# Sharing the exponents of the decays between GpSimd and VectorE, by block of columns

## What is computed

```python
# SSD, one direction:
acum = cumsum(dt * A)                            # per head
seg  = exp(where(mask, acum[l] - acum[s], NEG))  # decay from token s to token l
y    = einsum(C B^T, seg, x*dt)
# mLSTM, one direction:
dmat = where(mask, b[t] - b[s] + i[s], NEG)
m_t  = maximum(b[t] + m, max_s dmat)
sc   = (q k^T) * exp(dmat - m_t)
h    = (sc v) / maximum(|sum sc|, exp(-m_t))
```

## Time and profile before

| | |
|---|---|
| median of 3 runs | 2776.45 us (2774.89 to 2777.18) |
| profiled execution, its own time | 2774.36 us |
| its span | 2772.6 us |
| TensorE matmul / weight load busy | 91% / 83% |
| VectorE, ScalarE, GpSimd busy | 65%, 52%, 11% |
| mean granted TensorE clock | 0.959 of full speed |

### The profile page before, as it was taken

How to read it: one execution, slowest core, us unless ns; L and a number is a source line. 1 busy time by engine, 2 the same in 40 slices (tenths; PEclk the granted TensorE clock), 3 DMA queues, 4 the chain that set the end, 5 groups by cost and what they waited for, 6 DMA issues and landing times.

```text
span 2772.6 us, 42149 instructions
## 1 busy us (share of the span) xinstructions
PE 2532.0 (91%) x17296; PEld 2310.7 (83%) x17296; DVE 1790.0 (65%) x2816; ACT 1431.5 (52%) x2077; POOL 314.8 (11%) x299
## 2 busy tenths in 40 slices
PE   8998999999989997978998989998978998989997
PEld 7887989878789896977996888996978996888986
DVE  4556676565666655567666676874667666676864
ACT  4546545455564543555554535654555554535653
POOL 0000000000000000000229400000000229400000
PEclk9999999999999999989999989999989998999999
DMA  6543455555335565523566435664523465435663
GB/s 224 162 142 94 146 176 192 193 159 149 113 109 190 161 193 168 149 85 107 149 187 162 141 122 164 191 200 151 151 82 110 146 187 162 141 123 168 193 196 110
DMA packets 358670, 426.24 MB, mean 154 GB/s; under 512 B 21176, under 2 KB 286862, under 8 KB 358478
## 3 DMA queue, kind: packets, MB, share of 16 engines
q1 hardware_dynamic: 342602, 401.95, 47.0%
q10 hardware_dynamic: 14068, 15.91, 2.5%
q0 software_dynamic: 1808, 5.69, 0.6%
HBM read 422.35 MB, written 1.15 MB: 153 GB/s over the span
## 4 chain that ended last, share of the span: by engine, by line
PE 69%; DVE 14%; ACT 7%; issue 4%; POOL 4%; DMA 2%; ACTq 0%; DVEq 0%; POOLq 0%
PE ps L112 66%; POOL sE L124 3%; ACT whi L118 3%; DVE wlo L121 3%; PE ps L115 2%; ACT hgKm L118 1%; DVE sE L121 1%; DVE hgA L148 1%; ACT E L118 1%; DVE hgQB L121 1%; DVE hgQF L121 1%; DVE hgkf L121 1%; DVE hgkb L121 1%; DVE E L124 1%; ACT L118 0%
## 5 line engine op out<-in xcount | busy, mean ns | idle before, releaser
L121 DVE TENSOR_TENSOR wlo<-wring,whi 128x1024 fp32r<-128x1024 f32 x768 | 932.7, 1227 | 630.9 <-ACT whi L118 630.4
L118 ACT ACTIVATE whi<-wring 128x1024 fp32r<-128x1024 f32 x768 | 801.6, 1052 | 439.0 <-PE ps L112 428.7
L112 PE MATMUL ps<-uT,whi 128*128 128x256 f32 x4896 | 879.8, 284 | 23.2 <-DVE uT L121 23.2
L112 PEld LDWEIGHTS ps<-uT,whi 128*128 128x128 f32 x4896 | 761.1, 192 | 31.2 <-issue 24.0
L112 PE MATMUL ps<-uT,wlo 128*128 128x256 f32 (+1 forms) x2448 | 688.3, 281 | 0.0
L112 PEld LDWEIGHTS ps<-uT,wlo 128*128 128x128 f32 (+1 forms) x2448 | 469.3, 192 | 0.0
L112 PE MATMUL ps<-xT,whi 128*128 128x256 f32 x2112 | 382.0, 285 | 0.3 <-DVE wlo L121 0.3
L112 PEld LDWEIGHTS ps<-xT,whi 128*128 128x128 f32 x2112 | 327.1, 191 | 6.4 <-issue 3.7
L112 PE MATMUL ps<-xT,wlo 128*128 128x256 f32 x1056 | 296.7, 281 | 0.0
L112 PE MATMUL ps<-whi,hid 128*128 128x512 f32 x864 | 269.0, 391 | 0.0
L112 PEld LDWEIGHTS ps<-xT,wlo 128*128 128x128 f32 x1056 | 201.2, 190 | 0.1
(11 more groups left out here) (369 smaller groups left out, 3590.6 us busy)
## 6 DMA issues: line engine op xcount, KB each, us to landing
wring<-in_w_in SPq DMA_DIRECT2D x346, 512.0 KB, 3.7
wring<-in_mlp_w SPq DMA_DIRECT2D x128, 512.0 KB, 4.3
wring<-in_w_up SPq DMA_DIRECT2D x88, 512.0 KB, 4.4
wring<-in_w_down SPq DMA_DIRECT2D x44, 512.0 KB, 4.4
wring<-in_w_branch SPq DMA_DIRECT2D x32, 512.0 KB, 3.4
wring<-in_w_out SPq DMA_DIRECT2D x32, 512.0 KB, 3.8
wring<-in_mem_w_kv SPq DMA_DIRECT2D x16, 512.0 KB, 5.4
wring<-in_w_br_ssd SPq DMA_DIRECT2D x16, 512.0 KB, 3.8
```

The costliest lines, as they stand in the source:

```text
L112: return self.e.matmul(*p, **k) if self.e else Nothing()
L118: return self.e.activation(*p, **k) if self.e else Nothing()
L121: return self.e.tensor_tensor(*p, **k) if self.e else Nothing()
```

## The change

The four (with the mask's two: six) GpSimd instructions of a head become two (three): it does the two blocks of 256 columns. The two diagonal blocks of 128 are done by VectorE, in new functions `ssd_decay` and `ml_decay` of its program, which the list calls at the same steps. They record an event of their own, `arg2`, and ScalarE's exponential waits for both. The spread's DMA, too, waits for both before it writes over a piece. The mask of mLSTM is one constant of 256 columns, which GpSimd adds in one instruction, and VectorE takes in the same `scalar_tensor_tensor` as the column.

```diff
@@ schedule, decays of ssd_scan and ml_scan
-                c.spread[h].freed = ("arg", l, h)
+                c.spread[h].freed = [("arg", l, h), ("arg2", l, h)]
...
-                c.spread[16 + h].freed = ("arg", l, 16 + h)
+                c.spread[16 + h].freed = [("arg", l, 16 + h), ("arg2", l, 16 + h)]
@@ scalar_program
-        for ev in [s.before] if s.before else [("stored", c.l), ("storedmax", c.l), ("emraw", c.l)]:
+        for ev in s.before or [("stored", c.l), ("storedmax", c.l), ("emraw", c.l)]:
...
     def ssd_decay(c, h, s, r):
         e.wait_ge(*at(("arg", c.l, h)))
+        e.wait_ge(*at(("arg2", c.l, h)))
         e.activation(s.ap, s.ap, ACT.Exp).then_inc(*up("act_decay", ("sE", c.l, h)))
...
     def ml_decay(c, h, s, r):
         e.wait_ge(*at(("arg", c.l, 16 + h)))
+        e.wait_ge(*at(("arg2", c.l, 16 + h)))
@@ vector_program
+    def ssd_decay(c, h, s, r):
+
+        e.wait_ge(*at(("spread", c.l, h)))
+        if s.before:
+            e.wait_ge(*at(s.before))
+        for d in range(2):
+            i, o, q = 16 * (1 - d) + h, 512 + 128 * d, 256 - 128 * d
+            x = e.tensor_scalar(s.ap[:, o:o + 128], r.ap[:, q:q + 128], c.ncum[:, d, i:i + 1], c.ldt[:, d, i:i + 1], ALU.add, ALU.min)
+        x.then_inc(*up("dve_arg", ("arg2", c.l, h)))
+
+    def ml_decay(c, h, s, r):
+        e.wait_ge(*at(("spread", c.l, 16 + h)))
+        if s.before:
+            e.wait_ge(*at(s.before))
+        for d in range(2):
+            i, o, q = 8 * (1 - d) + h, 512 + 128 * d, 256 - 128 * d
+            x = e.scalar_tensor_tensor(out=s.ap[:, o:o + 128], in0=r.ap[:, q:q + 128], scalar=c.R[:, d, i:i + 1],
+                                       in1=K.NUL[:, 128 - 128 * d:256 - 128 * d], op0=ALU.add, op1=ALU.add)
+        x.then_inc(*up("dve_arg", ("arg2", c.l, 16 + h)))
@@ gpsimd_program
-        for o, w, q, st, d in blocks:
-            i = 16 * d + h
-            x = e.tensor_scalar(s.ap[:, o:o + w], r.ap[:, q:q + w], c.ncum[:, st, i:i + 1], c.ldt[:, st, i:i + 1], ALU.add, ALU.min)
+        for d in range(2):
+            i, o = 16 * d + h, 256 * d
+            x = e.tensor_scalar(s.ap[:, o:o + 256], r.ap[:, o:o + 256], c.ncum[:, d, i:i + 1], c.ldt[:, d, i:i + 1], ALU.add, ALU.min)
...
-        for o, w, q, st, d in blocks:
-            x = e.tensor_scalar(s.ap[:, o:o + w], r.ap[:, q:q + w], c.R[:, st, 8 * d + h:8 * d + h + 1], None, ALU.add)
+        for d in range(2):
+            i, o = 8 * d + h, 256 * d
+            x = e.tensor_scalar(s.ap[:, o:o + 256], r.ap[:, o:o + 256], c.R[:, d, i:i + 1], None, ALU.add)
         x.then_inc(*up("pool_arg"))
         e.wait_ge(*now("pool_arg"))
-        for v, mask in ((two(s.ap, 0, 640), K.NU), (two(s.ap, 384, 128), K.NL)):
-            x = e.tensor_tensor(v, v, mask.rearrange("p (s l) -> p s l", s=1).to_broadcast([128, 2, 128]), ALU.add)
-        x.then_inc(*up("pool_arg", ("arg", c.l, 16 + h)))
+        v = two(s.ap, 0, 384)
+        e.tensor_tensor(v, v, K.NUL.rearrange("p (s l) -> p s l", s=2), ALU.add).then_inc(*up("pool_arg", ("arg", c.l, 16 + h)))
```

More of the change, by code:

```diff
@@ L359, in layout @@
     K.L = [cst[:, C_L + 128:C_L + 384], cst[:, C_L:C_L + 256]]
-    K.mask, K.NU, K.NL = cst[:, C_U + 128:C_L + 256], cst[:, C_NU:C_NU + 128], cst[:, C_NL:C_NL + 128]
+    K.mask, K.NUL = cst[:, C_U + 128:C_L + 256], cst[:, C_NU:C_NL + 128]
     K.spread = nc.dram_tensor("spread", (DEPTH, 48, 256), F32, kind="Internal").ap()
@@ L2407, in vector_program @@
                  ml_max_step=ml_max_step, ml_max_negate=ml_max_negate, ml_max_cols=ml_max_cols, forget_out=forget_out, hg_start=hg_start,
-                 hg_products=hg_products, hg_split=hg_split, hg_scale=hg_scale, hg_norm=hg_norm, ssd_conv=ssd_conv, ssd_products=ssd_products, ssd_weights=ssd_weights,
+                 hg_products=hg_products, hg_split=hg_split, hg_scale=hg_scale, hg_norm=hg_norm, ssd_conv=ssd_conv, ssd_products=ssd_products, ssd_decay=ssd_decay, ml_decay=ml_decay, ssd_weights=ssd_weights,
                  ssd_outputs=ssd_outputs, ssd_norm=ssd_norm, ml_weights=ml_weights, ml_outputs=ml_outputs, ml_norm=ml_norm,
@@ L2454, in hg_merge @@
         e.tensor_copy(half(Qm), half(B.W.QB)).then_inc(*up("pool_hg", ("hgQB", B.tag, j)))
-    blocks = ((0, 256, 0, 0, 0), (256, 256, 256, 1, 1), (512, 128, 256, 0, 1), (640, 128, 128, 1, 0))
     def ssd_decay(c, h, s, r):
```

## The result

The changed kernel took 2821.97 us in the median of four runs (2819.22 to 2829.9), the kernel before 2776.81 beside it (2774.89 to 2787.96; the prediction's 2776.45 is the median without the last of these four runs): a ratio of 1.0159 [1.0125, 1.0192]. It is 1.6%, some 45 us, slower. The sign and the ring came out as forecast; the SSD's term was too small by 4 us a layer, and the mLSTM's was right in its sum, not in its parts.

The account below looks back on a forecast made before the run. GpSimd's exponents were taken to pace the SSD scans, VectorE's place in the order after the change. SSD's 5.5 plus mLSTM's 12 us a layer, 35 us in two, gave 2811.5 us, 1.3% slower; range 2775 to 2834.

Parts of the forecast that it names:

- the ring: Circle of waits in a scan step: VectorE's arguments, ScalarE's exponential and whi, VectorE's wlo, weights and outputs, next arguments.
- the SSD's term: SSD scan: 5.5 us a layer slower, 2.5 from heads 4 to 15 (68.8 against 66.3) and 3.0 from the start.
- GpSimd leaves the chain: SSD scans: GpSimd's work per head falls from 5.5 to 2.5 us, so it no longer sets the pace.
- The start: SSD scan's beginning: VectorE makes the first heads' exponents late, so head 4's exponential comes 3.0 us later.
- The mLSTM term: mLSTM scan: six steps at 2.59 us more plus 0.5, 16.0, less 4.1 already waited: 12 us a layer slower.
- named as a sign: Profile mark for a right forecast: the mLSTM steps grow by 2 us or more.
- Queues at nothing: Waits for the spread's DMA and the sE piece, and SyncE's slipping loads, were expected to add no cost of their own.
- The clock: TensorE's granted clock, not in the sum: more idle time could cost 8.7 us a layer, 17 in all.
- A: Rival: VectorE reaches the exponents early enough and TensorE's idle time is won, 2761.6 us; chance 11%.
- B: Rival: TensorE's panels in stock hide the mLSTM's later wlo, only SSD's 11 us stay, 2787.5 us; chance 12%.
- C: Rival: VectorE and GpSimd exclude each other, each head's first VectorE argument waits 1.25 us, 60 more, 2871 us; chance 4%.
- D: Rival: gain and ring cancel, nothing comes of the change, 2776 us; chance 5%.

Follow-up runs that it names:

- e3: Changed kernel, but VectorE's pairs write to an unread scratch tile and the exponential waits for GpSimd alone: 2757.27 us, 0.9904 of the kernel before.
- e5: Changed kernel with only VectorE's pairs moved earlier in its order, the first ones ahead of the scan; all waits kept: 2763.12 us, 0.9954 of the kernel before.
- e6: Changed kernel with only ScalarE's exponential moved behind the first whi of its step; all waits kept: 2754.7 us, 0.992 of the kernel before.
- e2: Changed kernel with SSD's exponents taken back to GpSimd, so only the mLSTM has the change: 2807.04 us, 1.0086 of the kernel before.
- e8: Changed kernel with both moves, VectorE's pairs earlier and ScalarE's exponential behind the first whi: 2739.05 us, 0.9864 of the kernel before.
- e9: Changed kernel without VectorE's pairs; GpSimd sets those columns to a constant and the exponential waits for it alone: 2756.96 us, 0.9908 of the kernel before.

## Why the prediction was right where it was, and where it was not

The forecast was 2811.5 us in a range of 2775 to 2834; measured were 2821.97.

- **GpSimd leaves the chain: right.** 4% became 0, and ScalarE's wait changed its releaser from POOL to DVE. That its busy time would fall by nearly half was wrong: 314.8 us became 204.3, a third less. Its instruction of 256 columns, taken at 1.25 us, has a mean of 1.55 in the changed kernel's largest group (48 instructions).
- **The ring in SSD: right in place and form, step by step.** Predicted and measured steps of heads 4 to 14, in us: 4.97 and 4.99, 8.48 and 8.73, 4.07 and 4.23, 5.93 and 6.14, 6.11 and 6.10, 5.51 and 5.72, 7.56 and 8.05, 8.48 and 8.66, 6.11 and 6.11, 5.51 and 5.69, 6.11 and 6.13. The pattern of the panels and copies holds everywhere; e3, e5 and e6, each of which opens the ring in another way, confirm the cause.
- **The size of the SSD term: this is the step that failed.** It was 5.5 us a layer, 2.5 for the steps and 3.0 for the start; measured were 9.1 and 9.8. The steps came to 70.55, not 68.8. Link by link, start to start on the two timelines, the pair makes about 0.9 of the 1.7 us: 0.60 us with its hop to ScalarE had been taken, from eight instructions in a row at 0.27 each. A pair alone ends only with the full length of its second instruction (a median of 342 ns): it measured 0.60 to 0.68, and from its start to the exponential's 0.69 to 0.78 (0.69 from 1460.33 to 1461.02, 0.77 from 1455.26 to 1456.03). The step with the norm has another 0.4, as the norm's instructions came 1.39 us after the weights, not 0.92. In step 7 the next exponential stood behind a square and a bank's copy on ScalarE, which the sum did not have there: 0.2. The weights' link, taken as 1.40, was 1.49 to 1.57 where outputs follow and 1.33 where they don't, 0.3 in all; so the steps 4, 8, 12 and 14 came within 0.02 of the forecast because a longer pair and shorter weights cancel there. The start came to 4.85 us, not 3.0, and here a term was missing, the larger part of the 1.85: the timeline above shows ScalarE's table load of 1.28 us *behind* the 3.55 us of waiting for the pair. In the kernel before it ran here:

```profile
1431.38 1.28 ACT L118 ACT_TABLE_LOAD   x1
```

That is ahead of the exponential at 1432.68, and nothing waited for it. The forecast moved the exponential behind VectorE's pair, and did not move the load that goes in front of it.
- **The mLSTM term: right in its sum, partly by luck.** + 12 us a layer forecast, 13.5 and 11.9 measured, 13.0 and 10.4 in e2 alone. wlo's wait for whi grew from 4.1 to 15.8 us (over 10 forecast), so the mechanism is the forecast one. But its place is another. The steps that were to pay 2.59 us each grew, from head 2's exponential to head 7's, by 0.0, 1.2, 2.1, 3.4 and 1.4 us in the first layer: 8.0 in five steps, and 7.4 in the second; only two of the five grew by the 2 us or more that was named as a sign. The two steps before them, put at nothing because TensorE would have panels ahead, grew by 2.0 and 1.7 (2.0 and 1.4), and the way from SSD's head 15 to mLSTM's head 0, which had no term, by 1.7 (1.1). What was left out and what was taken too high cancel.
- **Queues at nothing: right.** Among VectorE's waits over the two scans there is none in front of a pair, neither for the spread nor for the piece; the spreads landed in 4.6 to 7.0 us, and the lead of three heads covers them.
- **The clock, left out of the sum.** In the changed kernel the granted clock was 0.91 over 1430 to 1531 us, where TensorE was busy for 82.80 of 101.00, and 0.88 over 1531 to 1660, where it was busy for 101.28 of 129.00; it was 0.94 in the earlier trace rows, and it is 1.00 in e8. These are means over stretches at 2.4 and at 1.2 GHz: in the changed kernel it was 1.00 from 1458 to 1482 us and 0.50 from 1450 to 1454. The windows that sum to the loss are measured with the clock in them, and the ring's links are nearly all of VectorE and ScalarE, so no separate term is needed to reach 45 us. How much of the mLSTM's 25 us is clock was not separated.
- **The sum.** 35.1 forecast and 45.2 measured. Of the 10 missing, 7.9 are SSD's (18.9 against 11), 1.3 the mLSTM's (25.3 against 24), 0.6 lies outside the scans, and 0.4 is the difference between the profiled spans (44.8) and the medians (45.2).

The rivals. **A** asked what happens if VectorE reaches the exponents early enough, and gave 2761.6: the change as it is doesn't do this, but e5, which makes it so, measured 2763.12 (0.9954). So a gain is there, and the order kept it away; that the two numbers agree is luck. A takes 13.0 us a layer off SSD and adds 5.6 in the mLSTM. In e5 SSD, from the wlo behind the masks to head 15, is 5.1 and 2.8 us shorter, and the stretch from there to mLSTM head 7 is 2.9 and 3.7 shorter, not longer. Only e8 takes 13 us off heads 4 to 15 (52.9 and 53.0 against 66.3 and 65.8). **B**, mLSTM hides the ring: refuted by e2, 24 us for this scan alone. **C**, the engines exclude each other and VectorE waits: refuted. Here are the instructions that write tile sE in the scans of the changed kernel, 1430 to 1660 us (ns min/median/max):

```profile
L124 POOL TENSOR_SCALAR sE<-mxb,sm x20: 918/1464/3059, 1454.9 to 1584.7; 128x256 f32<-128x256 f32 x20
L124 DVE TENSOR_SCALAR sE<-mxb,sm x16: 337/342/546, 1437.5 to 1519.9; 128x128 f32<-128x128 f32 x16
...
L130 DVE SCALAR_TENSOR_TENSOR sE<-mxb,sm,cst x8: 338/346/823, 1546.1 to 1601.5; 128x128 f32<-128x128 f32 x8
```

Of the 32 instructions of SSD's 16 pairs the slowest took 546 ns (the other half, from the other pieces of the spread, at most 499); one that waits for a whole GpSimd instruction would show over 1000. Of the mLSTM's 16 one took 823 ns, and one 825 in the second layer: VectorE did wait there. They start at 1551.87 and 2402.07, 0.05 us after a GpSimd instruction of 0.73 us (1551.82 and 2402.02) that adds the mask, and end 0.14 us after its end. That costs about 0.5 us a layer, not C's 30. It is GpSimd's that vary, from 918 to 3059. The rule of the Trainium skill that was weighed here (SBUF — State Buffer, "Who interferes with whom": the later one waits for the whole of the other) fits these two, and may lie behind GpSimd's maxima, but not behind VectorE's other times; no run here separates it. **D**, gain and ring cancel: refuted by the ratio and its interval.

## What to carry to other kernels

A part of a head's work that is moved to a less busy engine is priced by where it comes in that engine's order, not by its length: the same 48 pairs cost 2.6 us as work and some 70 us as a link, because ScalarE's next panel was queued behind the wait for them and VectorE's next pair behind that panel. Before such a move, write down what is queued behind the new wait on its engine, and who feeds the instruction that is waited for; where that closes a circle, move the producer earlier or the consumer later in the same edit, as e8 does. Everything that the waiting instruction draws with it moves as well, such as a table load in front of an activation.

## What the runs showed that was not expected

- A `tensor_scalar` of VectorE with two operands per partition took 321 ns on the mean for 128 x 2 elements and 370 for 128 x 128: between these two sizes the columns cost next to nothing. And eight of them in a row take 0.27 us each, while a pair takes 0.60 to 0.68: in both, the price of the chain is a pace of some 0.26 for all but the last, plus the full length of the last (340 ns in the norm, 342 in the pair).
- GpSimd's instructions of 256 columns grew longer when the four blocks became two. In the group by shape over the whole run, this one (the mxb tiles) had a mean of 1.28 us in the kernel before, and 1.246 in the stretch of the earlier trace rows. The first line is the changed kernel's, the second that of e9, in which VectorE's pairs are gone:

```profile
L124 POOL TENSOR_SCALAR sE<-mxb,sm 128x256 f32<-128x256 f32 x48 | 74.0, 1550 | 89.9 <-PE ps L112 89.8
```

```profile
L124 POOL TENSOR_SCALAR sE<-mxb,sm 128x256 f32<-128x256 f32 x48 | 67.8, 1420 | 0.0
```

So at most about half of the 0.27 us (0.13) comes from the pairs; where the rest comes from wasn't tried. It ate a fifth of the relief of 3.0 us a head that the forecast had given GpSimd (2 x 0.27), at no cost here, since GpSimd was no longer on the path.
